# A mixer's weighted values on GpSimd in place of VectorE, in a two-layer diffusion backbone

## Chip and metric

The kernel runs on one core of a Trainium2 chip. The metric is the device time of one execution in microseconds (us), median of several runs. Profiles are of one execution each.

## The reference

Two layers of a backbone work on 512 latent and 256 context rows of width 1024. Each layer is a half-step SwiGLU feed-forward sublayer, a mixer, and another feed-forward sublayer. The mixer has Fourier channel groups and four bidirectional mLSTM heads. What matters here is how a head's states are made from its values, once for each direction:

```python
def mlstm_states(k, v, ig, lf, state0):
    ...
    a = b_tot[..., None] - b + igc
    m_loc = jnp.max(a, axis=-1)
    w = jnp.exp(a - m_loc[..., None])
    c_loc = jnp.einsum("bhcsd,bhcse->bhcde", vc * w[..., None], kc)
    n_loc = jnp.einsum("bhcs,bhcse->bhce", w, kc)

    def step(carry, xs):
        ...
        c_new = dec[..., None, None] * c_st + inj[..., None, None] * cl
        n_new = dec[..., None] * n_st + inj[..., None] * nl
```

`vc * w[..., None]` is the product that the change is about: 128 rows x 6 chunks x 129 columns (128 values and a column of ones that carries `n_loc`), for each head and each direction.

## The kernel before

Every engine has its own instruction stream, written out by hand in the block of that engine (`block.tensor`, `block.scalar`, `block.vector`, `block.gpsimd`, `block.sync`), and the streams meet only at semaphores (`S[...]`). The order on an engine is the order of the code. Matrix products with float32 data are split into a high and a low part; `split_w` makes them from each weight slot, the high part on ScalarE (L1387), the low part on VectorE (L1744).

The program runs six sublayers in a row: feed-forward, mixer, feed-forward for layer 0 and the same for layer 1. Mixer m (0 and 1) first projects its input and prepares gates; meanwhile GpSimd folds the Fourier inputs of four heads (`fold`, L1298 to L1322) and then has nothing to do until the next feed-forward sublayer (`rebuild`, L1335, then `sums`, L1348 to L1353). Then the four heads follow one another. For head h:

- TensorE (`mixer_pe`) projects q, k, k by token and v by token (`project`, L997 and L1001), does part of the Fourier products (`transform`, L1106), the products of q and k (`likeness`, L1031), and for h > 0 the transposes of the head before (`head_out`, L904). Then come the maxima (L1017, L1019), `added(h, 0)` (L1044), the Fourier products `dft` (L1088, L1091), `added(h, 1)`, the maxima of the other direction, and `inter` and `intra` (L1055, L1068) of both. `added(h, d)` multiplies k by the weighted values `wv[:, d]`, five chunks, and waits for `wv_sb`.
- ScalarE (`mixer_act`) copies the projections out of PSUM (L595); the last copy writes `vtok`, the values by token. Its semaphore is `qkv_sb`. In head 0 of each mixer it then makes the high part of a weight slot (`split(8)`, L1387). For h > 0 it takes the standard deviations of the head before (L614), which VectorE waits for in `normed`.
- VectorE (`mixer_dve`): for h > 0 it normalises the head before (`normed`, L856 and L858), which releases `head_out`. Then it makes the two weighted values (`values`, L784). Then `mixed` (L867) for the head before, or in head 0 the low part of the weight slot (L1744). Then `states(h, 0)` (L795, five steps, waits for `added(h, 0)`), `scores` (L809), `states(h, 1)`, `scores`, then `gather` and `combine` (L819 to L850), the last of which signals `hvar`.

`wv` (two directions of 6 x 129 columns) shares its memory with `num`, in which `gather` and `combine` work (`num = wv`, L395). The head's weights `wst` are ready before head 0 (semaphore `g_w`); the column of ones in `vtok` is written before it too (`nm_sel` comes behind it).

The stream of the heads on VectorE:

```python
            for h in range(HEADS):
                if h:
                    normed(h - 1)
                values(h, 0)
                values(h, 1)
                if h:
                    mixed(h - 1)
                else:
                    split(8)
                states(h, 0)
```

Of the kernel before, what the change touches and what calls it, by code (L numbers as in the profile page):

```python
# [24 lines left out]
ALU = mybir.AluOpType  # L25
# [3 lines left out]
P = 128  # L29
# [4 lines left out]
NT, NTL = TOK // P, SEQ // P  # L34
# [3 lines left out]
HEADS, HD = 4, 128  # L38
# [7 lines left out]
HV = HD + 1  # L46
# [134 lines left out]
def build(nc, x_in, w_ada0, w_ada_t, c_row_in, w_ff_in, w_ff_out, w_in, w_gates, w_out, w_qkv, cvec_in, gate_b_in,  # L181
          b_col_in, nw_col_in, nw_out_in, convw_in, convb_in, hn_w_in, fmix_in, dft_l_in, dft_c_in, dft_g_in, tri_in, x_out, gate_out_rows, nm_store, out):
    ctx = ExitStack()
    with ctx:
# [173 lines left out]
        def small(n, which="gate", end=A_DFTG):  # L358
            place[which] += n
            assert place[which] <= end  # L360
            return at(place[which] - n, n)
# [22 lines left out]
        wi, em, wst = (small(48).rearrange("p (d t h) -> p d t h", d=2, t=NT) for _ in range(3))  # L384

        def head(n):
            return small(n, "head", XN)
# [3 lines left out]
        vtok = head(NT * HV).rearrange("p (t n) -> p t n", t=NT)  # L391
        wv = head(2 * NT * HV).rearrange("p (d t n) -> p d t n", d=2, t=NT)
# [13 lines left out]
        S = {}  # L406
# [240 lines left out]
        def mixer_dve(dve, own, sub, split_w, first_out):  # L647

            m, n0, l = sub["mix"], sub["slot"], sub["l"]
# [6 lines left out]
            def split(s):  # L656
                split_w(n0 + s, (n0 + s) % 2, KC * 16 if s == 2 else SLOT)
# [119 lines left out]
            split(7)  # L777
            gates_arg()

            def values(h, d):  # L780

                if d == 0:
                    dve.wait_ge(S["qkv_sb"], 4 * (4 * m + h) + 4)
                nc.vector.tensor_tensor(wv[:, d], vtok, wst[:, d, :, h].unsqueeze(2).to_broadcast([P, NT, HV]), ALU.mult).then_inc(S["wv_sb"], 1)  # L784

            def states(h, d):

                md = 2 * (4 * m + h) + d
                if h:

                    dve.wait_ge(S["io_mm"], md - 1)
                dve.wait_ge(S["cloc_mm"], md + 1)
                for k in range(NT - 1):
                    col = scan_col(d, k, h)
                    ins = nc.vector.scalar_tensor_tensor(out=cst[:, d, k + 1, :], in0=cst[:, d, k, :], scalar=dec[:, col:col + 1],  # L795
                                                         in1=ps[:, 4 + k // 3, (k % 3) * HV:(k % 3 + 1) * HV],
                                                         op0=ALU.mult, op1=ALU.add)
                    if k < NT - 2:
                        link(ins)
                ins.then_inc(S["cst_sb"], 1)  # L800
# [52 lines left out]
            def normed(h):  # L853

                dve.wait_ge(S["hstd"], 4 * m + h + 1)
                link(nc.vector.reciprocal(den[:, 0, 1, 0:n_out], den[:, 0, 0, 0:n_out]))  # L856
                for t in range(n_out):
                    ins = nc.vector.tensor_scalar(hsum(h)[:, t, :], hsum(h)[:, t, :], mv[:, t, 0:1], den[:, 0, 1, t:t + 1], ALU.subtract, ALU.mult)  # L858
                ins.then_inc(S["hn"], 1)

            def mixed(h):

                dve.wait_ge(S["hnT"], 4 * m + h + 1)
                for g in range(2):
                    w = sub["groups"][g] * P
                    mg = mixT[:, g, 4 + h, 0:w]
                    ins = nc.vector.scalar_tensor_tensor(out=mg, in0=ps[:, 6 + g, 0:w], scalar=hn_w[:, l, h:h + 1], in1=mg,  # L867
                                                         op0=ALU.mult, op1=ALU.mult)
                ins.then_inc(S["mix_done"], 1)
# [6 lines left out]
            for h in range(HEADS):  # L876
                if h:
                    normed(h - 1)
                values(h, 0)
                values(h, 1)  # L880
                if h:
                    mixed(h - 1)
                else:
                    split(8)
                states(h, 0)
                scores(h, 0)
                if h == HEADS - 1:
                    first_out(sub)
                states(h, 1)
                scores(h, 1)  # L890
                gather(h, 0)
                gather(h, 1)
                combine(h)
# [376 lines left out]
        def _(pool):  # L1270
# [8 lines left out]
            def fold(sub, h):  # L1279
# [44 lines left out]
                steps.wait()  # L1324
                pool.sem_inc(S["folded"], 1)

            adds = Count(pool, S["s_add"])

            def rebuild(sub):
# [31 lines left out]
            for sub in SUBS:  # L1361
                if sub["kind"] == "ffn":
                    par0 = sub["slot"] % 2
                    rebuild(sub)
                    sums(sub, 0, par0, first=True)
                    sums(sub, 1, 1 - par0, second=True)
                    with adds.loop(ST // 2 - 1, 4) as i:
                        for s in range(2):
                            sums(sub, i * 2 + (2 + s), (par0 + s) % 2)
                if sub["kind"] == "mix":  # L1370
                    for h in range(HEADS):
                        fold(sub, h)


        @block.scalar
# [1062 lines left out]
```

## Time and profile before

| | us |
|---|---|
| three timed runs: median | 2498.82 |
| lowest, highest | 2495.97, 2498.97 |
| span of the profiled execution, first to last instruction | 2494.0 |
| TensorE busy in it | 2427.1 (97%) |
| VectorE busy | 1874.1 (75%) |
| ScalarE busy | 1126.9 (45%) |
| GpSimd busy | 611.6 (25%) |

The profiled execution's own time is known as its span; the timed median lies 4.8 us above it. The granted TensorE clock was 0.997 of full speed over the span. The heads of the first mixer lie at about 688 to 795 us of the span, those of the second at about 1990 to 2077. In the rows PE is TensorE, DVE VectorE, ACT ScalarE, POOL GpSimd. A row of a timeline gives the start and the length of a run of like instructions (xN of them), and in brackets how long the engine had been idle before and what ended that. `arena` is one large buffer, in which `vtok`, `wv`, `wt`, `cst` and others are pieces; `ps` is PSUM.

### The profile page before, as it was taken

The page shows a single profiled execution, that of the slowest core. Times are in us where ns is not written, and L with a number is a line of the kernel's source. Part 1 is how long each engine was busy: PE and PEld are TensorE (multiplying, and loading weights), DVE is VectorE, ACT ScalarE, POOL GpSimd, SP SyncE. Part 2 cuts the span into 40 slices and gives each one's busy share as a digit, 9 for nine tenths or more (in the row PEclk, how much of TensorE's full clock was granted, in tenths as well). Part 3 has the DMA queues.
Part 4 walks back from the last instruction along what each step waited for, and adds up shares of the span by engine and source line. Part 5 has one row for each costly group of instructions (what it writes and reads, how often), then busy time and mean ns, then how long its engine had stood idle before and what let it go on. Part 6 is the DMA issues. An engine that isn't in the chain of part 4 may idle for free.

```text
span 2494.0 us, 35459 instructions
## 1 busy us (share of the span) xinstructions
PE 2427.1 (97%) x13552; PEld 2208.6 (89%) x13552; DVE 1874.1 (75%) x2362; ACT 1126.9 (45%) x1627; POOL 611.6 (25%) x429
## 2 busy tenths in 40 slices
PE   7999999999999999999999999999999998899998
PEld 4999998888977899999888999999889777899987
DVE  5799997776567779988766799876556677898733
ACT  5334443444453743443354544443444555555522
POOL 0344440000500034544000145541000500266400
PEclk9999999999999999999999999999999999999999
DMA  6333336543111343333643423346443203322331
GB/s 258 110 127 127 140 135 256 186 148 94 52 48 36 118 160 122 129 111 132 247 161 135 169 110 126 130 156 242 180 142 101 89 28 118 136 101 101 119 118 67
DMA packets 100369, 328.33 MB, mean 132 GB/s; under 512 B 7810, under 2 KB 38050, under 8 KB 86946
## 3 DMA queue, kind: packets, MB, share of 16 engines
q1 hardware_dynamic: 83040, 316.33, 35.5%
q10 hardware_dynamic: 17218, 10.55, 1.4%
q8 instruction: 68, 1.11, 0.2%
q14 instruction: 43, 0.34, 0.0%
HBM read 318.28 MB, written 8.57 MB: 131 GB/s over the span
## 4 chain that ended last, share of the span: by engine, by line
PE 78%; DVE 12%; issue 5%; ACT 3%; DMA 2%; POOL 0%; SPq 0%; ACTq 0%; DVEq 0%; POOLq 0%
PE ps L2206 29%; PE ps L2166 27%; PE ps L2154 8%; PE ps L928 6%; DVE junk L1764 3%; DVE w_all L2014 2%; DMA acc<-w_ada_t 1%; DVE w_all L1744 1%; PE ps L2248 1%; PE ps L997 1%; PE ps L1068 1%; PE ps L1044 1%; PE ps L2258 1%; PE ps L952 1%; PE ps L1055 1%
## 5 line engine op out<-in xcount | busy, mean ns | idle before, releaser
L2206 PE MATMUL ps<-w_all,hj_all 128*128 128x512 f32 x2856 | 655.6, 391 | 4.9 <-DVE arena L828 2.5
L2206 PEld LDWEIGHTS ps<-w_all,hj_all 128*128 128x128 f32 x2856 | 535.1, 188 | 117.9 <-DVE arena L828 2.9
L2166 PE MATMUL ps<-xn_hi,w_all 128*128 128x384 f32 (+1 forms) x2592 | 612.2, 318 | 12.0 <-DVE gate_row L2067 11.1
L1744 DVE TENSOR_TENSOR w_all<-raw,w_all 128x2048 fp32r<-128x2048 f32 x138 | 322.0, 2333 | 268.8 <-ACT w_all L1387 268.7
L2166 PEld LDWEIGHTS ps<-xn_hi,w_all 128*128 128x128 f32 x2592 | 449.3, 189 | 18.9 <-DVE gate_row L2067 18.0
L2166 PE MATMUL ps<-xn_lo,w_all 128*128 128x384 f32 (+1 forms) x1296 | 411.0, 317 | 0.0
L1387 ACT ACTIVATE w_all<-raw 128x2048 fp32r<-128x2048 f32 x139 | 262.6, 1889 | 241.4 <-PE ps L2206 206.1
L2014 DVE TENSOR_TENSOR w_all<-raw,w_all 128x1024 fp32r<-128x1024 f32 (+1 forms) x216 | 329.9, 1529 | 36.5 <-ACT w_all L1609 36.2
L1764 DVE SCALAR_TENSOR_TENSOR junk<-acc,silu_row 128x1024 bf16<-128x1024 f32 x224 | 325.7, 1454 | 16.4 <-DMA acc<-w_ada_t 7.1
L1609 ACT ACTIVATE w_all<-raw 128x1024 fp32r<-128x1024 f32 (+1 forms) x216 | 197.9, 918 | 261.1 <-PE ps L2166 241.9
L2154 PE MATMUL ps<-xn_hi,w_all 128*128 128x384 f32 (+1 forms) x1024 | 245.7, 324 | 9.9 <-DVE xn_lo L1822 7.6
L2166 PEld LDWEIGHTS ps<-xn_lo,w_all 128*128 128x128 f32 x1296 | 245.1, 189 | 0.0
L2166 PE MATMUL ps<-t,w_all 128*128 128x384 f32 x1296 | 233.3, 334 | 0.0
L2166 PEld LDWEIGHTS ps<-t,w_all 128*128 128x128 f32 x1296 | 225.4, 188 | 0.0
L1613 ACT ACTIVATE gate_row<-ps 128x384 f32<-128x384 f32 (+1 forms) x216 | 100.3, 464 | 262.0 <-PE ps L2166 262.0
L2154 PEld LDWEIGHTS ps<-xn_hi,w_all 128*128 128x128 f32 x1024 | 180.2, 190 | 11.3 <-DVE xn_lo L1822 7.8
L1335 POOL TENSOR_TENSOR arena<-xn_hi,xn_lo 128x1536 f32<-128x1536 f32 (+1 forms) x8 | 27.7, 3488 | 637.5 <-DVE xn_lo L1822 637.5
L1348 POOL TENSOR_TENSOR w_sum<-raw 128x512 f32<-128x512 f32 x68 | 103.2, 1518 | 286.3 <-DMA raw<-w_ff_in 206.2
L1353 POOL TENSOR_TENSOR raw<-raw,w_sum 128x512 f32<-128x512 f32 x68 | 134.1, 1971 | 147.4 <-DVE w_all L2014 147.0
L928 PE MATMUL ps<-xn_hi,w_all 128*128 128x384 f32 (+1 forms) x640 | 165.1, 349 | 2.9 <-DVE xn_lo L1822 2.9
L2154 PE MATMUL ps<-xn_lo,w_all 128*128 128x384 f32 (+1 forms) x512 | 165.1, 322 | 0.0
L2166 PE MATMUL ps<-hj_all,w_all 128*128 128x384 f32 (+1 forms) x864 | 149.9, 321 | 2.3 <-ACT gate_row L1613 2.3
(236 smaller groups left out, 3213.0 us busy)
## 6 DMA issues: line engine op xcount, KB each, us to landing
raw<-w_ff_in SPq DMA_DIRECT2D x104, 1024.0 KB, 4.9
raw<-w_ff_out SPq DMA_DIRECT2D x77, 1024.0 KB, 5.0
acc<-w_ada_t SPq DMA_DIRECT2D x128, 512.0 KB, 3.3
raw<-w_out SPq DMA_DIRECT2D x16, 1024.0 KB, 4.9
raw<-w_in SPq DMA_DIRECT2D x12, 1024.0 KB, 5.7
x<-x_in SPq DMA_DIRECT2D x12, 512.0 KB, 10.7
gate_row<-gate_out_rows ACTq DMA_DIRECT2D x12, 512.0 KB, 6.4
x_out<-x SPq DMA_DIRECT2D x12, 512.0 KB, 9.0
```

Of the source, the lines that this page charges most:

```text
L928: ins = mm(ps[:, ch if ch < 4 else ch % 3 + 3 * g, 0:wd], w[:, k, c * P:(c + 1) * P], xx[:, k, g * GW:g * GW + wd], start=(k == 0 and i == ...
L1348: adds.link(nc.gpsimd.tensor_tensor(s21[:, 1, :], a21, a22, ALU.add))
L1353: nc.gpsimd.tensor_tensor(a12, a12, s21[:, 0, :], ALU.subtract).then_inc(S["s_sum"], 1)
L1387: nc.scalar.activation(w_hi[par][:, 0:width], raw[par][:, 0:width], ACT.Copy).then_inc(S["w_hi"], 1)
L1609: ins = nc.scalar.activation(pair_out(par0, i, 0), pair_raw(par0, i, raw[r], first), ACT.Copy)
L1613: nc.scalar.activation(fast_tmp(sub, i), ps[:, bank_, 0:sub["wide"]], ACT.Copy).then_inc(S["snap"], 1)
L1744: nc.vector.tensor_tensor(w_lo[par][:, 0:width], raw[par][:, 0:width], w_hi[par][:, 0:width].bitcast(F32), ALU.subtract).then_inc(S["w_lo" ...
L1764: ins = nc.vector.scalar_tensor_tensor(out=junk[:], in0=acc[:].rearrange("p a n -> p (a n)"), scalar=1.0, in1=silu_row[:, s, :], op0=ALU.m ...
L2014: ins = nc.vector.tensor_tensor(pair_out(par0, i, 1), pair_raw(par0, i, raw[r], first), pair_out(par0, i, 0).bitcast(F32), ALU.subtract)
L2154: ins = mm(ps[:, 4 * b + part + c, col:col + wd], w[:, k, c, :], xx[:, k, t0:t0 + wd], start=(k == 0 and i == 0), stop=(k == KC - 1 and i ...
L2166: ins = mm(ps[:, bank_, 0:xx[0].shape[-1]], w[:, c], x_[:, k, :], start=start and k == 0 and a == 0, stop=k == 3 and a == 2, skip_group_ch ...
L2206: ins = mm(ps[:, 2 * i + hf, :], xx[:, i * P:(i + 1) * P], w[:, c, hf * 512:(hf + 1) * 512], start=first and c == 0 and a == 0, stop=last ...
```

## The change

The two products of each head are taken out of VectorE's stream and put into GpSimd's, behind the four folds of the mixer. GpSimd waits once for `nm_sel` and `g_w`, and for each head for the values (`qkv_sb`) and, from the second head on, for `hvar` of the head before, since `num` and `wv` are the same memory. The arithmetic, the order on the other engines and the memory are unchanged.

```diff
--- before.py
+++ after.py
@@ -777,12 +777,6 @@
             split(7)
             gates_arg()
 
-            def values(h, d):
-
-                if d == 0:
-                    dve.wait_ge(S["qkv_sb"], 4 * (4 * m + h) + 4)
-                nc.vector.tensor_tensor(wv[:, d], vtok, wst[:, d, :, h].unsqueeze(2).to_broadcast([P, NT, HV]), ALU.mult).then_inc(S["wv_sb"], 1)
-
             def states(h, d):
 
                 md = 2 * (4 * m + h) + d
@@ -876,8 +870,6 @@
             for h in range(HEADS):
                 if h:
                     normed(h - 1)
-                values(h, 0)
-                values(h, 1)
                 if h:
                     mixed(h - 1)
                 else:
@@ -1324,6 +1316,15 @@
                 steps.wait()
                 pool.sem_inc(S["folded"], 1)
 
+            def values(sub, h, d):
+
+                k = 4 * sub["mix"] + h
+                if d == 0:
+                    pool.wait_ge(S["qkv_sb"], 4 * k + 4)
+                    if k:
+                        pool.wait_ge(S["hvar"], k)
+                nc.gpsimd.tensor_tensor(wv[:, d], vtok, wst[:, d, :, h].unsqueeze(2).to_broadcast([P, NT, HV]), ALU.mult).then_inc(S["wv_sb"], 1)
+
             adds = Count(pool, S["s_add"])
 
             def rebuild(sub):
@@ -1370,6 +1371,11 @@
                 if sub["kind"] == "mix":
                     for h in range(HEADS):
                         fold(sub, h)
+                    pool.wait_ge(S["nm_sel"], sub["mix"] + 1)
+                    pool.wait_ge(S["g_w"], sub["mix"] + 1)
+                    for h in range(HEADS):
+                        values(sub, h, 0)
+                        values(sub, h, 1)
 
 
         @block.scalar
```

On VectorE at a later head of the first mixer stood (s_hnT is signalled by the transposes of the head before, s_cloc_mm by `added`):

```order
L850 BN_AGGR arena<-arena 128x2 x5
L856 RECIPROCAL arena<-arena 128x6 [waits s_hstd]
L858 TENSOR_SCALAR arena<-arena 128x128 [waits s_dve]
L858 TENSOR_SCALAR arena<-arena 128x128 x5
L784 TENSOR_TENSOR arena<-arena 128x774 [waits s_qkv_sb]
L784 TENSOR_TENSOR arena<-arena 128x774
L867 SCALAR_TENSOR_TENSOR arena<-ps,hn_w,arena 128x384 [waits s_hnT]
L867 SCALAR_TENSOR_TENSOR arena<-ps,hn_w,arena 128x384
L795 SCALAR_TENSOR_TENSOR arena<-arena,ps 128x129 [waits s_cloc_mm,s_io_mm]
```

and now stands (line numbers of the changed kernel, L850 and L852 being `normed`, L861 `mixed`, L789 `states`):

```order
L844 BN_AGGR arena<-arena 128x2 x5
L850 RECIPROCAL arena<-arena 128x6 [waits s_hstd]
L852 TENSOR_SCALAR arena<-arena 128x128 [waits s_dve]
L852 TENSOR_SCALAR arena<-arena 128x128 x5
L861 SCALAR_TENSOR_TENSOR arena<-ps,hn_w,arena 128x384 [waits s_hnT]
L861 SCALAR_TENSOR_TENSOR arena<-ps,hn_w,arena 128x384
L789 SCALAR_TENSOR_TENSOR arena<-arena,ps 128x129 [waits s_cloc_mm,s_io_mm]
```

The two rows of 774 columns between `normed` and `mixed` are gone; nothing else moved.

On GpSimd, between the last fold of the first mixer (L1318 to L1322) and the `rebuild` of the next feed-forward sublayer stood:

```order
L1318 TENSOR_TENSOR junk<-arena 128x127 [waits s_fold]
L1320 TENSOR_TENSOR arena<-arena 128x127 [waits s_fold]
L1322 COPY arena<-junk 128x127 [waits s_fold]
L1335 TENSOR_TENSOR arena<-xn_hi,xn_lo 128x1536 [waits s_fold,s_xn_done]
L1335 TENSOR_TENSOR arena<-xn_hi,xn_lo 128x1536
L1348 TENSOR_TENSOR arena<-raw 128x512 [waits s_w_raw1]
```

and now stands (L1310 to L1314 is the end of the last fold, L1326 the products of heads 0 and 1, and then those of heads 2 and 3, which read like those of head 1):

```order
L1310 TENSOR_TENSOR junk<-arena 128x127 [waits s_fold]
L1312 TENSOR_TENSOR arena<-arena 128x127 [waits s_fold]
L1314 COPY arena<-junk 128x127 [waits s_fold]
L1326 TENSOR_TENSOR arena<-arena 128x774 [waits s_fold,s_qkv_sb,s_g_w,s_nm_sel]
L1326 TENSOR_TENSOR arena<-arena 128x774
L1326 TENSOR_TENSOR arena<-arena 128x774 [waits s_hvar,s_qkv_sb]
L1326 TENSOR_TENSOR arena<-arena 128x774
...
L1336 TENSOR_TENSOR arena<-xn_hi,xn_lo 128x1536 [waits s_xn_done]
L1336 TENSOR_TENSOR arena<-xn_hi,xn_lo 128x1536
```

Eight products of each mixer stand there now, each head's pair behind one wait of its own.

## Rows read from the trace of the kernel before

**Rows 1.** The page, part 4: the chain that ended last, by engine.
```profile
PE 78%; DVE 12%; issue 5%; ACT 3%; DMA 2%; POOL 0%; SPq 0%; ACTq 0%; DVEq 0%; POOLq 0%
```

**Rows 2.** Timeline, first mixer, head 0: start us, us, engine, line [idle before <-releaser].
```profile
697.85 1.91 ACT L1387 ACTIVATE w_all<-raw 128x2048 fp32r<-128x2048 f32 x1
...
698.06 1.84 DVE L784 TENSOR_TENSOR arena<-arena 128x774 f32<-128x774 f32 x2 [9.59 <-ACT arena L595]
699.82 2.28 DVE L1744 TENSOR_TENSOR w_all<-raw,w_all 128x2048 fp32r<-128x2048 f32 x1
...
699.48 1.38 PE L1044 MATMUL ps<-arena 128*128 128x129 f32 x10
...
702.43 1.03 PE L1091 MATMUL ps<-arena 128*128 128x256 f32 x4
704.05 1.35 PE L1044 MATMUL ps<-arena 128*128 128x129 f32 x10 [0.59 <-DVE arena L795]
```

**Rows 3.** Timeline, first mixer, head 1.
```profile
719.73 1.61 ACT L595 ACTIVATE arena<-ps 128x384 f32<-128x384 f32 x4
...
720.08 1.63 DVE L858 TENSOR_SCALAR arena<-arena 128x128 f32<-128x128 f32 x6
...
725.28 0.73 DVE L795 SCALAR_TENSOR_TENSOR arena<-arena,ps 128x129 f32<-128x129 f32 x2 [0.77 <-PE ps L1044]
...
721.86 0.84 PE L904 MATMUL ps<-ident,arena 128*128 128x128 f32 x6 [0.34 <-DVE arena L858]
...
723.79 1.38 PE L1044 MATMUL ps<-arena 128*128 128x129 f32 x10
...
727.60 1.28 PE L1044 MATMUL ps<-arena 128*128 128x129 f32 x10
```

**Rows 4.** Timeline, first mixer: from a ScalarE evacuation to GpSimd's first fold.
```profile
626.12 0.87 ACT L515 ACTIVATE arena<-ps 128x384 f32<-128x384 f32 x2 [6.37 <-PE ps L928]
...
627.06 0.45 POOL L1298 TENSOR_TENSOR junk<-arena 128x127 f32<-128x127 f32 x1 [259.11 <-ACT arena L515]
```

**Rows 5.** Timeline, second mixer, head 1.
```profile
2016.81 1.63 ACT L595 ACTIVATE arena<-ps 128x384 f32<-128x384 f32 x4
...
2017.15 1.12 DVE L858 TENSOR_SCALAR arena<-arena 128x128 f32<-128x128 f32 x4
...
2020.23 0.87 DVE L867 SCALAR_TENSOR_TENSOR arena<-ps,hn_w,arena 128x256 f32<-128x256 f32 x2
```

**Rows 6.** Chain in order of time, second mixer, head 1: start us, us, what.
```profile
2019.98 1.33 PE ps L1044 x10
...
2021.40 0.36 DVE arena L795
...
2023.43 1.35 PE ps L1044 x10
```

**Rows 7.** GpSimd's tensor_tensor by line: duration ns min/median/max.
```profile
L1299 POOL TENSOR_TENSOR junk<-arena x8: 410/778/2457, 627.5 to 1974.0; 128x127 f32<-128x127 f32 x8
L1348 POOL TENSOR_TENSOR w_sum<-raw x68: 1282/1295/2378, 116.5 to 2342.0; 128x512 f32<-128x512 f32 x68
L1358 POOL TENSOR_TENSOR w_all<-raw,w_all x1: 4502/4502/4502, 38.3 to 38.3; 128x2048 fp32r<-128x2048 f32 x1
```

**Rows 8.** Timeline: GpSimd and VectorE at work at the same time, at two places.
```profile
1061.32 1.28 POOL L1349 TENSOR_TENSOR raw<-raw 128x512 f32<-128x512 f32 x1
1062.57 2.27 POOL L1350 TENSOR_TENSOR w_sum<-w_sum,raw 128x512 f32<-128x512 f32 x1
...
1061.36 2.33 DVE L2014 TENSOR_TENSOR w_all<-raw,w_all 128x1024 fp32r<-128x1024 f32 x1 [0.62 <-ACT w_all L1609]
...
1977.79 2.49 POOL L1309 TENSOR_TENSOR arena<-junk 128x127 f32<-128x127 f32 x4
...
1979.77 0.58 DVE L744 TENSOR_SCALAR arena<-arena 64x128 f32<-64x128 f32 x1
1980.39 0.28 DVE L745 TENSOR_SCALAR arena<-arena 64x128 f32<-64x128 f32 x1
```

## Prediction

> **What bounds the kernel now.** I read the page's chain first [rows 1]. TensorE carries 78% of it, VectorE 12%, GpSimd nothing. So time taken off VectorE counts only where TensorE waits for it, and I went on to the operation that moves. It is L784, 16 times by the code: a pair in each of four heads in each of two mixers. A pair takes 1.84 us [rows 2], so 14.7 us (8 x 1.84) is the most that the change could give. Then I read the timeline around three places: the first head of the first mixer [rows 2], a later head of it [rows 3], a later head of the second mixer [rows 5, 6]. The reader is to look there for who is waited for at the end of each wait.
>
> In a later head of the first mixer ScalarE ends its four copies of k and v at 721.34 (719.73 + 1.61) [rows 3]. VectorE finishes the six L858 at 721.71, does the pair of products, then L867, and then sits idle 0.77 us until TensorE's L1044 releases L795 at 725.28. So VectorE has spare time right behind the products. TensorE starts L1044, the reader of the first product, at 723.79 with no wait before it, and reads the second product only at 727.60. In the second mixer the same L795 waits too: L867 ends at 2021.10 (2020.23 + 0.87) [rows 5] and the chain runs from L1044 at 2019.98 to L795 at 2021.40 and back to L1044 at 2023.43 [rows 6]. There the chain passes the reader of the first product with nothing to spare on its way to the states.
>
> **What leaving VectorE gives.** In six of the eight heads (all but the first of each mixer) L867 moves up to when its transposes are done, and L795 then waits longer for TensorE. L867 was in time before, so nothing is gained. In the first head of a mixer the pair runs 698.06 to 699.90 and is followed by the split L1744 at 699.82 [rows 2]. But that split also needs ScalarE's L1387, which ends at 699.76 (697.85 + 1.91). With the pair gone it could start at about 699.80, at best 0.1 us earlier, two times. I take 0.
>
> **What a product costs on GpSimd.** No row has this shape on GpSimd. Its plain tensor_tensor took 1.282 us at best for 512 columns and 4.502 us for 2048 [rows 7]. The line through them is 0.209 us + 2.096 ns a column, so 774 columns take 1.83 us, against 0.92 on VectorE (half a pair). One input is a broadcast column and the pattern has six pieces, which may shift it. From below it can't be under the 512-column row, 1.28. From above I take the rate of the 127-column row, 0.410 us / 127 x 774 = 2.50. I take 1.83, since two rows of the same engine on both sides of 774 give it. The Trainium skill ("GPSIMD Engine Reference", section 3.1) gives about 2.6 cycles an element at 1.2 GHz: 1.68 us as an estimate without the dispatch. By it the delay below would be 1.1 us in place of 1.5.
>
> **When it starts and ends.** GpSimd's first fold started 0.07 us after ScalarE's L515 ended (626.12 + 0.87 = 626.99, then 627.06) [rows 4]. I take 0.08. From VectorE's last L858 (721.71) to TensorE's L904 it is 0.15 in [rows 3]; I use 0.14 for GpSimd too.
>
> Second mixer, later heads: the copies end at 2018.44 (2016.81 + 1.63) [rows 5]. The product runs 2018.52 to 2020.35, and TensorE can start at 2020.49. It started at 2019.98 [rows 6]. That is 0.51 late, on the chain, for heads 1, 2 and 3: **+1.5 us**. The second product ends at 2022.2 and is read at 2023.43, so it is hidden with 1.1 to spare. L795 waits 0.51 longer too, so the loss passes whole to the next L1044.
>
> First mixer, later heads: copies end 721.34, the product would start 721.42, while the last L858 is still running until 721.71. Suppose it is held off until then (see the lock below): it ends at 721.71 + 1.83 - 0.13 = 723.41, TensorE can go at 723.55, and it went at 723.79 [rows 3]. **0**, with 0.24 to spare. The second ends near 725.2, read at 727.60. **0**.
>
> First head of both mixers: VectorE's pair started 698.06, so GpSimd's first product runs about 698.05 to 699.88. TensorE's L1044 then starts at 700.02 in place of 699.48, and the Fourier products behind it (L1088, L1091), which ended at 703.46, move by no more than that, to 704.0. That is still ahead of the L1044 at 704.05, which waits 0.59 for L795 anyway [rows 2]. The split L1744 comes at 699.80 and meets GpSimd's last columns; the second product waits behind it to 702.1 and ends at 702.10 + 1.70 = 703.80, readable at 703.94 against 704.05. **0 to +0.1 each**, I take 0.
>
> The added waits on GpSimd stand in front of the `rebuild` of the next feed-forward sublayer alone, which waits for rows made after the mixer's output product, so nobody is held up behind them. No DMA moves, and SyncE's queue is untouched.
>
> **The lock.** The trace shows that the two engines exclude each other. GpSimd's 512-column operation at 1061.32 took its plain 1.28; VectorE's split of 0.04 us later took 2.33, ending 1.09 after it; the next GpSimd operation, at 1062.57, took 2.27, ending 1.15 after the split [rows 8]. The second to come waits for the first to end, and hides 0.13 of its own start. Single-input operations are in it too: L744 took 0.58 with GpSimd's L1309 running, and L745, of the same shape, 0.28 when it was over [rows 8]. The Trainium skill ("SBUF — State Buffer", section "Who interferes with whom") states it as an exclusive lock in which issue order decides who blocks, and counts tensor_scalar from memory to memory and two-input operations among those that take it; by that rule, L858 and L1744 contend and L867, L795 and L809 (one input in PSUM) don't. The trace agrees as far as those rows go.
>
> **Sum.** 0 (VectorE's relief) + 0 (first mixer) + 1.5 (second mixer) = +1.5 us on a span of 2494.0. The timed median of the runs is 2498.82, 4.8 us above the span; I add the 1.5 to it: 2500.3.
>
> **Rivals.**
> 1. *GpSimd wins the lock over the split in the first head.* Its second product is issued about 0.05 before its first ends (1062.57 against 1062.60 shows 0.03), so at 699.83 to 699.85, and the split comes at 699.80 to 699.82. If the product comes first it runs to 701.67 and the split ends at 701.67 + 2.15 = 703.82 in place of 702.10: +1.7 twice, total +4.9, 2503.7. A product a few hundredths shorter than 1.83 decides it. At the lower end, 1.28, the split would end at 702.7 and the whole be +1.2. Chance 0.14.
> 2. *Slower: GpSimd comes between the L858.* The six start about 0.26 apart, the last at 721.37 (721.71 - 0.34). GpSimd asks at 721.42. If it is served ahead of the sixth (it decides if the copies' signal arrives 0.05 us earlier, or if the sixth asks only when the fifth has ended at 721.45), the sixth ends at 721.42 + 1.83 + 0.21 = 723.46, 1.75 late. TensorE's transposes L904 wait for it on the chain, three times: +5.2, total +6.7, 2505.5. In the second mixer the four L858 end at 2018.27, ahead of the copies, so it doesn't occur. Chance 0.12.
> 3. *The product is slow on GpSimd,* at 2.50: second mixer 1.18 x 3, first mixer 0.43 x 3, first heads 2 x 1.1: +7.0, 2505.8. The total passes 5 us at about 2.3 us a product. Chance 0.06.
> 4. *Faster:* the relief of VectorE counts after all, because TensorE's next work waits on VectorE by something the chain put on another engine. At most 14.7. Idle time right after the pair in every head I looked at speaks against it. Chance 0.03.
> 5. *My forecast,* +0.5 to +3: 0.60. No change at all, because the product is 1.3 us long or the slack is larger: 0.05.
>
> **How the numbers follow.** About 0.2% (5.0 us here) is what a measurement can tell from no change. Over it lie rival 2 (0.12), half of rival 3 (0.03) and a third of rival 1, which stands at 4.9 (0.04): slower 0.18 or so. Faster 0.03. The rest, 0.79, is no change. The three timed runs lie 3.0 us apart, so I put 1.5 below and above. Low 2497: no change at all less noise. High 2506: rivals 1 and 2 with it, and most of 3.
>
> **What would show it.** L784's successor appears on GpSimd 16 times, median near 1.83 (1.7 to 2.0; more where the lock held it). TensorE idles about 0.5 us ahead of its first added products in the second mixer, released by GpSimd, and not in heads 1 to 3 of the first. The time from head to head stays in the first mixer and grows by 0.5 us in the second. Wrong would be: a L858 of 2 us; the split L1744 of a first head taking 4 us; or a head's period getting shorter.

## The result and the profile after

| | median us | runs | ratio to the kernel before, 95% interval |
|---|---|---|---|
| before | 2498.89 | 4 | |
| changed | 2510.51 (2505.99 to 2514.59) | 4 | 1.0051 [1.0037, 1.0065] |

The change costs 0.5%, 11.6 us. The forecast was 2500.3, with 2506 as its upper end. It was wrong in size and in the likeliest case: two collisions that it had given small chances both happened, and the clock, which no case had, fell.

The profiled execution took 2512.26 us; its span is 2510.3, 16.3 us more than that of before. Its page (busy times, chain by engine) reads:

```profile
PE 2437.0 (97%) x13552; PEld 2217.6 (88%) x13552; DVE 1866.8 (74%) x2346; ACT 1126.6 (45%) x1627; POOL 634.1 (25%) x445
...
PE 77%; DVE 12%; issue 5%; ACT 3%; DMA 2%; POOL 0%; SPq 0%; DVEq 0%; ACTq 0%; POOLq 0%
```

The chain looks as it did [rows 1]. VectorE lost only 7.3 us of busy time (1874.1 before) though 14.7 us of products left it, and TensorE gained 9.9 (2427.1 before) with the same 13552 matmuls. Both are signs of instructions that took longer, so I looked for those. The product itself, by its line (duration ns min/median/max), was shorter than forecast:

```profile
L1326 POOL TENSOR_TENSOR arena<-arena x16: 1483/1486/1522, 700.6 to 2072.5; 128x774 f32<-128x774 f32 x16
```

To place the loss I cut both traces at the same two events: the first L989 (L997 before) of a mixer, and the first L2212 (L2206 before) of its output product. The windows of the kernel before first, with one inner stretch that is needed below. The columns are start and end, length, busy time and count of PE, PEld (weight loads), DVE, ACT and POOL, the granted clock PEclk, DMA share and GB/s:

```profile
688.76:785.14 96.38, 92.71 (x626) 76.81 (x626) 71.64 (x180) 48.64 (x118) 0.00 (x0) 1.00 0.09 32
767.47:770.47 3.00, 2.66 (x20) 1.98 (x18) 3.00 (x8) 2.30 (x4) 0.00 (x0) 1.00 0.00 0
1990.60:2068.80 78.20, 74.16 (x500) 61.08 (x501) 58.74 (x162) 41.31 (x94) 0.00 (x0) 1.00 0.11 39
```

And the changed kernel, with four inner stretches:

```profile
core 0: us, PE busy (x) PEld busy (x) DVE busy (x) ACT busy (x) POOL busy (x), PEclk, DMA share, GB/s
691.25:795.55 104.30, 96.02 (x626) 79.30 (x626) 69.93 (x172) 48.63 (x118) 11.83 (x8) 0.97 0.09 29
775.00:778.00 3.00, 1.47 (x9) 0.98 (x9) 1.97 (x3) 1.00 (x1) 2.75 (x2) 1.00 0.00 0
778.30:784.70 6.40, 6.40 (x20) 5.32 (x21) 2.93 (x8) 1.66 (x6) 0.00 (x0) 0.50 0.00 0
2000.88:2083.50 82.62, 76.64 (x500) 63.41 (x500) 53.13 (x154) 41.30 (x94) 11.73 (x8) 0.96 0.11 37
2013.00:2017.00 4.00, 1.63 (x12) 1.26 (x11) 3.33 (x8) 0.66 (x2) 0.00 (x0) 1.00 0.41 129
2017.20:2023.80 6.60, 6.60 (x28) 5.60 (x27) 4.01 (x11) 1.14 (x4) 0.00 (x0) 0.50 0.18 71
```

The first mixer grew from 96.38 to 104.30 us, the second from 78.20 to 82.62: 12.3 us together, and the median rose by 11.6. In the profile the rest of the span grew by 4.0 more (2319.4 to 2323.4); a second profile of the same kernel (run after2 below) has 12.4 in the mixers and -0.8 outside, so those 4.0 aren't the change. Outside the mixers, too, TensorE has stretches of 3.4 us at a granted clock of 0.50: four in this profile, its start and end apart (from 358.2, 2092.2, 2126.3 and 2382.3), two in that of before (2110.1 and 2366.1), two in after2 (804.2 and 2377.7).

Three things make up nearly all of the 12.3.

**The sixth normalisation.** Timeline of the first mixer, head 1 (compare [rows 3]). The third and fourth rows are the same line in later windows, which show its last two instructions and its last one alone; the fifth shows the first product of the pair alone:

```profile
723.33 1.61 ACT L595 ACTIVATE arena<-ps 128x384 f32<-128x384 f32 x4
...
723.68 2.94 DVE L852 TENSOR_SCALAR arena<-arena 128x128 f32<-128x128 f32 x6
...
724.71 1.90 DVE L852 TENSOR_SCALAR arena<-arena 128x128 f32<-128x128 f32 x2
...
724.97 1.65 DVE L852 TENSOR_SCALAR arena<-arena 128x128 f32<-128x128 f32 x1
...
725.01 1.52 POOL L1326 TENSOR_TENSOR arena<-arena 128x774 f32<-128x774 f32 x1 [21.46 <-ACT arena L595]
...
726.76 0.85 PE L896 MATMUL ps<-ident,arena 128*128 128x128 f32 x6 [1.65 <-DVE arena L852]
```

ScalarE's copies end at 724.94 and GpSimd's product starts at 725.01. VectorE's sixth L852 is on record from 724.97, 0.04 earlier, and yet it takes 1.65 us where the others take 0.34, and ends 0.09 after the first product (726.53). The fifth, begun at 724.71, runs until 725.05, past the product's start, and the product takes 1.52 us where the products that meet nothing take 1.483 to 1.491. So it reads as if the product waited those 0.03 to 0.04 for the fifth to end and was served then, ahead of the sixth. It is the same in all fifteen heads of the five profiles in which the sixth took 1.65 (products of 1.515 to 1.522 us); no run shows the engines' requests themselves. TensorE's L896 waits 1.65 us in place of 0.34. The six at 748.57 and 773.45 show the same 2.94. A head lasts 24.88 us from one L852 to the next in place of 23.57. That is +1.31 three times, 3.9 us.

**The split of slot 8.** Timeline of the first heads of both mixers (compare [rows 2]); the last row is the kernel before, second mixer:

```profile
700.34 1.91 ACT L1393 ACTIVATE w_all<-raw 128x2048 fp32r<-128x2048 f32 x1
...
702.07 1.49 POOL L1326 TENSOR_TENSOR arena<-arena 128x774 f32<-128x774 f32 x1
...
702.34 3.37 DVE L1750 TENSOR_TENSOR w_all<-raw,w_all 128x2048 fp32r<-128x2048 f32 x1 [11.37 <-ACT w_all L1393]
...
707.65 1.35 PE L1036 MATMUL ps<-arena 128*128 128x129 f32 x10 [1.51 <-DVE arena L789]
...
2015.95 1.43 PE L1036 MATMUL ps<-arena 128*128 128x129 f32 x10 [2.37 <-DVE arena L789]
...
2004.51 1.35 PE L1044 MATMUL ps<-arena 128*128 128x129 f32 x10 [1.85 <-DVE arena L795]
```

In the second mixer the split took 3.42 us. In the first the second product starts at 702.07, when the split L1750 isn't ready, as ScalarE's L1393 ends at 702.25. VectorE gets going at 702.34 and the split takes 3.37 us in place of 2.28. From the mixer's start to this L1036 it is 16.40 us (707.65 - 691.25) in place of 15.29, and 15.07 in place of 13.91 in the second mixer: +1.1 and +1.2.

**TensorE's clock.** The windows show what no case of the forecast had: 6.4 us at a granted clock of 0.50, which is 1.2 GHz where 1.00 is 2.4, in the fourth head of the first mixer, and 6.6 us in the second mixer behind its L1036. Ahead of them TensorE was busy 1.47 of 3.00 us and 1.63 of 4.00. In the kernel before it was busy 2.66 of 3.00 us at the place that answers to the first (767.47, the same distance ahead of its L904), and 2.15 of 4.00 at the place that answers to the second (2001.56), with a granted clock of 1.00 at both. Its matmuls in the slow stretch of the first mixer:

```profile
778.72 2.52 PE L1036 MATMUL ps<-arena 128*128 128x129 f32 x10
781.03 3.62 PE L1080 MATMUL ps<-arena 128*128 128x256 f32 x8
```

In the other heads these two take 1.38 and 1.89, so 2.87 us less. What the clock cost can be read from the matmuls' starts. From the fourth head's L896 (776.53) to its second L1036 (785.53) it is 9.00 us, and 5.76 in the heads at full clock: 3.24 us. In the second mixer it is 16.74 us from the late L1036 (2015.95) to the next L896 (2032.69), and 13.90 between the same two in the kernel before (2004.51, 2018.41): 2.84 us.

In the second mixer, heads 1 to 3 are 19.15 us long in place of 18.99. The chain there (start us, us, what), against [rows 6]:

```profile
2032.79 1.50 POOL arena L1326
...
2034.34 1.40 PE ps L1036 x10
```

TensorE follows the product's end by 0.04. So 82.62 - 78.20 = 4.42 is 0.5 for these three heads, 1.2 for the split and 2.8 for the clock, to within 0.1.

One small gain stands against this. At the end of the first mixer, VectorE sits idle before its last L828, the last operation ahead of the output product. In the kernel before:

```profile
784.06 1.03 DVE L828 TENSOR_TENSOR arena<-arena,ps 128x387 f32<-128x387 f32 x2 [0.78 <-PE ps L1068]
```

In the changed kernel its idle time there is 0.41 in place of 0.78, and the output product starts 0.37 us sooner. The same 0.41 stands in every other run below but b_early, also in b_delay and b_delay2, whose products are on VectorE; so it isn't the product's leaving that did it. What did wasn't traced.

The whole: 3.9 + 2.3 + 0.5 + 6.1 - 0.4 = 12.4 of the 12.3, with each term read on its own.

### The profile page after: what moved, and what is told of

Same layout as the page of the kernel before. It is cut to its first block, busy times and chain, and to the rows that moved or that the text cites. A ratio compares the mean times of both kernels' runs of the same rounds, so it can differ in the third digit from the quotient of the medians.

```text
span 2510.3 us, 35466 instructions
## 1 busy us (share of the span) xinstructions
PE 2437.0 (97%) x13552; PEld 2217.6 (88%) x13552; DVE 1866.8 (74%) x2346; ACT 1126.6 (45%) x1627; POOL 634.1 (25%) x445
## 4 chain that ended last, share of the span: by engine, by line
PE 77%; DVE 12%; issue 5%; ACT 3%; DMA 2%; POOL 0%; SPq 0%; DVEq 0%; ACTq 0%; POOLq 0%
PE ps L2212 29%; PE ps L2172 27%; PE ps L2160 8%; PE ps L920 6%; DVE junk L1770 3%; DVE w_all L2020 2%; DVE w_all L1750 1%; DMA acc<-w_ada_t 1%; PE ps L2254 1%; PE ps L989 1%; PE ps L1036 1%; PE ps L1060 1%; PE ps L1047 1%; PE ps L944 1%; ACT w_all L1393 1%
## 5 line engine op out<-in xcount | busy, mean ns | idle before, releaser
L2212 PE MATMUL ps<-w_all,hj_all 128*128 128x512 f32 x2856 | 657.1, 391 | 4.6 <-DVE arena L822 2.2
L2212 PEld LDWEIGHTS ps<-w_all,hj_all 128*128 128x128 f32 x2856 | 536.4, 189 | 117.8 <-DVE arena L822 2.5
L1750 DVE TENSOR_TENSOR w_all<-raw,w_all 128x2048 fp32r<-128x2048 f32 x138 | 324.0, 2348 | 291.1 <-ACT w_all L1393 291.0
L1393 ACT ACTIVATE w_all<-raw 128x2048 fp32r<-128x2048 f32 x139 | 262.6, 1889 | 243.8 <-PE ps L2212 202.5
```

Source lines behind the costliest of these rows:

```text
L1393: nc.scalar.activation(w_hi[par][:, 0:width], raw[par][:, 0:width], ACT.Copy).then_inc(S["w_hi"], 1)
L1750: nc.vector.tensor_tensor(w_lo[par][:, 0:width], raw[par][:, 0:width], w_hi[par][:, 0:width].bitcast(F32), ALU.subtract).then_inc(S["w_lo" ...
L2212: ins = mm(ps[:, 2 * i + hf, :], xx[:, i * P:(i + 1) * P], w[:, c, hf * 512:(hf + 1) * 512], start=first and c == 0 and a == 0, stop=last ...
```

## The experiments

Two questions were open: are the two collisions the cause, and is the slow clock their consequence or an accident? All ratios are to the kernel before on the same chip.

**a_hn.** GpSimd waits for the normalisations.

```
             if k:
                 pool.wait_ge(S["hvar"], k)
+                if h:
+                    pool.wait_ge(S["hn"], k)
```

> The changed kernel, with one more wait on GpSimd: from head 1 on, a product starts only when VectorE has normed the head before (its six L852 instructions are through), so that it can't come between them. Theory A (the two engines contend for the pair of ports, and TensorE's clock falls as a consequence of its longer waits): the six take 1.63 us again in place of 2.94, the first mixer's heads last 23.6 to 24.1 us in place of 24.9, the granted clock at the fourth head of the first mixer is 1.00 in place of 0.50 at the 7 us around 778 us, so the first mixer shrinks from 104.3 us to 97.5 to 99; the second mixer stays at 82.6 with its slow clock; in all 4 to 7 us below the changed kernel, near 2505. Rival B (the clock falls for a reason that has nothing to do with the product's place): the six are short again, but a stretch at 0.50 stays in the first mixer, which lasts 100 to 101. Rival C (the product's own 1.49 us on GpSimd against VectorE's is what costs): the heads stay at 24.9, since the product now even starts later.

Measured: 2502.28 us, ratio 1.0022 [1.0012, 1.0032], by the ratios some 7 us under the changed kernel. Timeline of head 1, then the window of the first mixer (columns as above):

```profile
719.75 1.63 DVE L852 TENSOR_SCALAR arena<-arena 128x128 f32<-128x128 f32 x6
...
721.52 0.85 PE L896 MATMUL ps<-ident,arena 128*128 128x128 f32 x6 [0.34 <-DVE arena L852]
...
721.55 2.93 POOL L1328 TENSOR_TENSOR arena<-arena 128x774 f32<-128x774 f32 x2 [21.93 <-DVE arena L852]
```

```profile
687.32:784.44 97.12, 92.77 (x626) 76.80 (x626) 66.02 (x172) 48.69 (x118) 11.73 (x8) 1.00 0.09 31
```

The six take 1.63 again, L896 waits 0.34, the heads last 23.57, and the clock in the first mixer is 1.00. The mixer, at 97.12 just under the 97.5 to 99 expected, is 7.2 us shorter, of which 3.9 are the six and 3.2 the clock. The product starts 0.17 after their end and is still in time. Theory A held, rivals B and C fell here. The second mixer, where nothing was changed, again lasted 82.62 us and kept its slow stretch, 6.4 us at 0.50 from 2008.2.

**a_split.** The second product of head 0 waits for the split.

```
+        if h == 0 and d:
+            pool.wait_ge(S["w_lo"], sub["slot"] + 8 + 1 + START)
         nc.gpsimd.tensor_tensor(wv[:, d], vtok, wst[...]..., ALU.mult)
```

> The changed kernel, with one more wait on GpSimd: in head 0 of each mixer the second product starts only when VectorE's split of slot 8 (L1750) is written. Theory A: L1750 takes 2.3 us again in place of 3.4, TensorE's wait at L1036 falls back from 1.51 to 0.6 us in the first mixer and from 2.37 to 1.9 in the second, 0.9 to 1.1 us a mixer; if the slow clock in the second mixer (0.50 at 2017 to 2024 us) is a consequence of that longer wait, it goes too, and the second mixer shrinks from 82.6 to 78.5 to 79.5 us; the first mixer's heads 1 to 3 stay as they are, with the slow clock at 778 us. In all 2 to 5 us below the changed kernel. Rival B: the slow clock in the second mixer stays, and that mixer lasts 81.5. Rival C: the late second product (near 2 us later) holds back what reads it, and nothing is gained.

Measured: 2504.33 us, 1.0033 [1.002, 1.0046]. Timeline of the first mixer's head 0, then windows of both mixers:

```profile
702.31 1.49 POOL L1328 TENSOR_TENSOR arena<-arena 128x774 f32<-128x774 f32 x1 [2.60 <-DVE w_all L1752]
...
699.94 2.29 DVE L1752 TENSOR_TENSOR w_all<-raw,w_all 128x2048 fp32r<-128x2048 f32 x1 [11.37 <-ACT w_all L1395]
...
704.18 1.35 PE L1036 MATMUL ps<-arena 128*128 128x129 f32 x10 [0.43 <-DVE arena L789]
```

```profile
688.86:790.48 101.62, 94.41 (x626) 78.27 (x626) 68.86 (x172) 48.63 (x118) 11.87 (x8) 0.98 0.09 30
1997.92:2076.61 78.69, 73.79 (x501) 60.87 (x501) 51.87 (x154) 41.30 (x94) 11.77 (x8) 1.00 0.11 38
```

The split is back at 2.29 us, TensorE waits 0.43 in place of 1.51 although the product now starts 2.6 us after the first one ended. The second mixer is 3.9 us shorter, 1.2 of it the split and 2.8 the clock, which stays at 1.00. In the first mixer the waits of 1.65 us remain, and so does a slow stretch, a shorter one (0.50 from 775.4 to 778.4; 101.62 is 1.6 us over the 96.06 of the run a_both below and the 3.9 of the six). The same kernel once more, one execution:

> The kernel whose second product of head 0 waits for the split, once more, for one look at the clock. Theory A: the waits of 1.65 us at L896 bring a stretch at 0.50 into the first mixer again (101.5 to 103.5 us), none into the second, which stays at 78.7. Rival B: the first mixer at 100 us, with 1.00, or the second with 0.50.

Measured: 2505.01 us, mixers of 101.62 and 78.68 us, a stretch of 0.50 again in the first (at 751 us this time), none in the second. Theory A.

**a_both.** Both waits.

> The changed kernel with both waits of the two runs before it: no product lies beside the split of head 0, none between the six normalisations. Theory A: the effects add, no stretch at 0.50 is left within either mixer; first mixer 96.4 to 98.5 us against 96.4 of the kernel before and 104.3 of the changed one, second 78.2 to 79.5 against 78.2 and 82.6; total 2499 to 2502, within 0.15% of the kernel before. Rival B: slow stretches stay in the mixers, 2503 to 2506. Rival C: 2508 or more.

Measured: 2495.20 us, 0.9992 [0.9983, 1.0001]. Windows of both mixers:

```profile
687.93:783.99 96.06, 92.78 (x627) 76.81 (x627) 64.93 (x172) 48.63 (x118) 11.76 (x8) 1.00 0.10 32
1989.42:2068.09 78.67, 73.79 (x500) 60.86 (x501) 51.87 (x154) 41.30 (x94) 11.77 (x8) 1.00 0.11 38
```

The mixers sum to 174.73 us against 174.58 of before: the whole loss is gone, with the products still on GpSimd. (The second is 0.5 longer, the first 0.3 shorter, by the 0.37 at its end told above.) The median lies 2.2 us under that of before and under the 2499 to 2502 that I expected, which the mixers don't explain and the interval doesn't confirm. The second mixer's 0.5 is the price of the GpSimd product, as forecast in kind.

**a_fill.** The collisions stay, TensorE gets work in its waits.

```
     if h:
         pe.wait_ge(S["xab_sb"], k + 1)
+        if m == 0:
+            for _ in range(4):
+                mm(ps[:, 6, 0:GW], kT[:, 0:P], qT[:, 0:GW], start=True, stop=True)
         head_out(pe, sub, h - 1)
...
     dft(h)
+    if h == 0:
+        pe.wait_ge(S["wt_sb"], 8 * m + 1)
+        for _ in range(4):
+            mm(ps[:, 2, 0:GW], kT[:, 0:P], qT[:, 0:GW], start=True, stop=True)
     added(h, 1)
```

> The changed kernel; on TensorE four matmuls of some 1.3 us in all, whose result nobody reads, stand in two of its waits: ahead of the head's output in the first mixer's heads 1 to 3, and ahead of L1036's wait in head 0 of both mixers. The collisions on VectorE stay (L852 2.94 us, L1750 3.4 us). Theory A: TensorE idles less before the places where the clock fell, so the granted clock stays at 1.00 at 778 us and at 2017 us and the matmuls L1036, L1080 and L1047 take 1.4, 1.9 and 1.2 us again; each mixer shortens by up to 2.9 us less what the extra matmuls add on the path (0 to 1.3 us each head), in all 0 to 5 us below the changed kernel. Rival B: the stretches at 0.50 stay where they were and the time rises by what the matmuls add.

Measured: 2508.97 us, 1.0053 [1.004, 1.0066]. Timeline of the two collisions, then windows of both mixers:

```profile
725.16 2.94 DVE L852 TENSOR_SCALAR arena<-arena 128x128 f32<-128x128 f32 x6
...
2011.72 3.42 DVE L1757 TENSOR_TENSOR w_all<-raw,w_all 128x2048 fp32r<-128x2048 f32 x1 [9.78 <-ACT w_all L1400]
```

```profile
691.89:796.00 104.11, 102.30 (x659) 82.74 (x659) 69.94 (x172) 48.69 (x118) 11.83 (x8) 1.00 0.08 29
2002.01:2081.82 79.81, 76.15 (x509) 62.39 (x509) 53.01 (x154) 41.34 (x94) 11.73 (x8) 1.00 0.11 38
```

The collisions are unchanged (2.94 and 3.42), but the clock is 1.00 in both mixers. In the second, where the extra matmuls fit into the wait, the mixer is 2.8 us shorter: the price of the clock by a second way. In the first they don't fit; each later head grew from 24.88 to 25.62 us, and the mixer stayed where it was, within 0.2. The median says as little: 11.6 us over the kernel before, as the changed kernel, though the mixers' windows come to 9.3. So this was no gain in time, but it separates the clock from the collisions.

**after2.** The changed kernel again, beside the runs that follow.

> The changed kernel once more, unaltered, on the same chip as the runs beside it. Theory A (the slow clock within the mixers follows from this kernel's waits): the profile shows 0.50 again in the fourth head of the first mixer or close to it, and in head 0 of the second; mixers of 104.3 and 82.6 us within 0.5. Rival B (the clock falls by chance): the stretches lie elsewhere or are gone, 101.4 and 79.8 us. Time within 2507 to 2513 in either case.

Measured: 2508.93 us, 1.0046 [1.0033, 1.0059]; mixers 104.28 and 82.67; 0.50 at 749.8 to 756.2 us (the third head this time, not the fourth) and at 2016.1 to 2022.5. The slow stretches recur with the same sum; only the head varies.

**b_delay.** The kernel before, no product on GpSimd, but VectorE late.

```
+    def spend():
+        nc.vector.tensor_tensor(gate_row[:, 1, :], silu_row[:, 0, :], silu_row[:, 1, :], ALU.mult)
     def normed(h):
         dve.wait_ge(S["hstd"], 4 * m + h + 1)
+        if m == 0 and h < HEADS - 1:
+            spend()
...
     else:
+        spend()
         split(8)
```

> The kernel before, all products on VectorE and GpSimd idle, with one more VectorE operation of 2 x 1024 values (some 1.2 us, its result isn't read) ahead of the six normalisations in the first mixer's heads 1 to 3 and ahead of the split of slot 8 in head 0 of both mixers. It gives TensorE waits as long as the collisions did, without GpSimd. Theory A (the clock falls because TensorE waits longer): TensorE's wait at L904 is 1.5 to 1.6 us in place of 0.34, each of these heads lasts 1.2 us longer, and stretches at a granted clock of 0.50 appear in the first mixer and in head 0 of the second: mixers of 103 to 105 and 82 to 82.5 us, time 2507 to 2512. Rival B (the clock falls for another reason, as power drawn by GpSimd beside VectorE): it stays 1.00 in the mixers, which last 101.0 to 101.5 and 79.2 to 79.6 us, time 2503 to 2505.

Measured: 2504.53 us, 1.0026 [1.0016, 1.0036]. Timeline of two waits, one in each mixer, then windows of both mixers and of a stretch in the second:

```profile
722.94 0.85 PE L911 MATMUL ps<-ident,arena 128*128 128x128 f32 x6 [1.48 <-DVE arena L864]
...
2008.28 2.49 PE L1051 MATMUL ps<-arena 128*128 128x129 f32 x10 [2.99 <-DVE arena L795]
```

```profile
687.57:788.12 100.55, 92.72 (x627) 76.80 (x627) 76.17 (x184) 48.69 (x118) 0.00 (x0) 1.00 0.09 30
1993.23:2076.71 83.48, 78.34 (x500) 64.94 (x500) 60.05 (x163) 41.34 (x94) 0.00 (x0) 0.94 0.11 36
2008.00:2017.40 9.40, 9.12 (x38) 8.06 (x39) 4.81 (x14) 1.14 (x4) 0.00 (x0) 0.50 0.28 107
```

Mixed. In the second mixer the longer wait (2.99 us at the line that waited 1.85) brings 9.4 us at 0.50, with GpSimd idle: its work isn't needed for it. In the first mixer three waits of 1.47 to 1.48 us and one of 1.72 in head 0 did not, and it lasted 100.55. My expectation of a slow stretch there was a miss, and so was that of the time, 2507 to 2512.

**b_delay2.** The same in the first mixer alone, with two such operations in each later head, one behind the other.

> The kernel before, products on VectorE and GpSimd idle, with two more VectorE operations of 1024 values ahead of the six normalisations in the first mixer's heads 1 to 4 (the fourth one falls in the tail) and nothing added in head 0. TensorE's wait at L904 becomes 0.34 + 2 x 1.2 = 2.8 us. Theory A (long waits of TensorE bring the slow clock, with or without GpSimd; 1.47 us did not suffice in the first mixer, 1.65 did): each of these heads lasts 26.0 to 26.2 us and at least one stretch at 0.50 lies in the first mixer, which lasts 96.4 + 7.4 + 1.5 to 6, so 105 to 110 us; the second mixer stays at 78.2 with a clock of 1.00. Rival B (the clock needs GpSimd's work beside VectorE's): 1.00 throughout the first mixer, 103.5 to 104.

Measured: 2514.99 us, 1.0060 [1.0036, 1.0084]. The wait in head 1 of the first mixer, then windows of both mixers and of one inner stretch:

```profile
725.40 0.85 PE L911 MATMUL ps<-ident,arena 128*128 128x128 f32 x6 [2.86 <-DVE arena L865]
```

```profile
689.79:803.74 113.95, 103.09 (x626) 84.35 (x626) 79.10 (x186) 48.68 (x118) 0.00 (x0) 0.90 0.08 27
726.70:733.10 6.40, 6.40 (x20) 5.06 (x20) 3.82 (x10) 1.66 (x6) 0.00 (x0) 0.50 0.00 0
2011.12:2089.32 78.20, 74.15 (x501) 61.08 (x501) 58.77 (x162) 41.34 (x94) 0.00 (x0) 1.00 0.12 39
```

Each of the three waits of 2.86 us is followed by a stretch at 0.50 (the second from 754.0 to 763.8, the third from 784.7 to 791.1), and the second mixer, left alone, is again 78.20 us at 1.00. The first grew by 17.6 us where the waits add 7.6; the rest, some 10, is the clock. Theory A's 105 to 110 was too low, as I had counted on fewer slow stretches.

**b_early.** The split itself: can it leave this place? With the products on VectorE as before, ScalarE does its part of the split of slot 8 after the second of its head's four copies, VectorE ahead of the head's products.

```
 ScalarE:   project(h, 1)
+           if h == 0: split(8)
            ...
            project(h, 3)
-           if h == 0: split(8)
 VectorE:  +split(8)
            dve.wait_ge(S["g_w"], m + 1)
            for h in range(HEADS):
                ...
-               else: split(8)
```

> The kernel before, with the split of slot 8 moved ahead in both mixers: ScalarE copies the high part before it evacuates slot 0's product pair of head 0 (where it idles 1.3 us), VectorE takes its own part ahead of head 0's products (where it idles 9.6 us). Nothing else is changed. Theory A (this split is what TensorE waits for behind L795): TensorE's waits at L1044 of head 0, 0.59 and 1.85 us, go to 0 to 0.6; first mixer 95.7 to 96.4 us against 96.4, second 76.4 to 77.7 against 78.2 (ScalarE's evacuations there come up to 1 us later); 1 to 2.4 us below the kernel before. Rival B: ScalarE's later evacuations cost what is gained, no difference.

Measured: 2496.02 us, 0.9994 [0.9985, 1.0003]. The split in the first mixer and TensorE's wait in the second, then windows of both mixers:

```profile
694.09 2.29 DVE L1743 TENSOR_TENSOR w_all<-raw,w_all 128x2048 fp32r<-128x2048 f32 x1 [6.29 <-ACT w_all L1386]
...
2003.10 1.35 PE L1043 MATMUL ps<-arena 128*128 128x129 f32 x10 [0.34 <-DVE arena L795]
```

```profile
688.08:783.73 95.65, 92.55 (x627) 76.97 (x627) 71.82 (x180) 48.59 (x118) 0.00 (x0) 1.00 0.09 32
1990.70:2067.40 76.70, 74.14 (x500) 61.07 (x501) 58.94 (x162) 41.12 (x94) 0.00 (x0) 1.00 0.11 39
```

The split runs while VectorE would be idle, TensorE waits 0.34 in place of 1.85 in the second mixer and not at all in the first. The mixers lose 0.7 and 1.5 us, 2.2 in all. The median fell by 1.6, within what can be told from nothing.

**a_early.** The same with the products on GpSimd, with a_hn's wait; neither collision can happen.

> The changed kernel (products on GpSimd) with the wait behind the six normalisations from head 1 on, and the split of slot 8 moved ahead as in the run beside it, so that neither collision can happen. Theory A: the products on GpSimd are then hidden in the first mixer and cost 0.15 us a head in the second; mixers of 95.5 to 96.3 and 76.8 to 78.2 us, no stretch at 0.50 in them, time within 1 us of the run that has the early split with the products on VectorE, 2495 to 2499. Rival B: 1.49 us a product on GpSimd against 0.92 on VectorE shows in head 0, where TensorE waits for both, and this version is 1 to 2 us above the other.

Measured: 2495.73 us, 0.9991 [0.9982, 0.9999]. The first mixer lasted 95.44 us; the window of the second:

```profile
1991.08:2068.93 77.85, 73.78 (x501) 60.87 (x501) 51.91 (x154) 41.08 (x94) 11.72 (x8) 1.00 0.12 39
```

As fast as the run before it; both medians lie under that of the kernel before by what can hardly be told from nothing. In the mixers' windows the two versions with the early split are 2.2 and 1.3 us shorter than the kernel before, wherever the product stands. They differ by GpSimd's price in the second mixer (77.85 against 76.70): 0.5 in heads 1 to 3, as before, and 0.6 in head 0, where TensorE's first L1035 waits 0.84 us for GpSimd, and waited 0.20 for VectorE.

## Why the prediction was wrong

- **Relief of VectorE worth nothing: right.** a_both, with all products gone from VectorE and no collision, has the mixers of before within 0.2 us: 0.5 for GpSimd's product in the second, less the 0.37 at the end of the first, which isn't the relief.
- **The product's cost: direction right, size off.** 1.49 us against 1.83. The line through two rows of other shapes was 0.34 too high. The lower estimate from the Trainium skill ("GPSIMD Engine Reference", section 3.1), 1.68, was nearer, also too high. The signal to TensorE took 0.04, not 0.14.
- **Second mixer, heads 1 to 3: right in kind.** Forecast +0.51 each, measured +0.16 (19.15 against 18.99), mostly the shorter product's doing. The prediction also took TensorE's start of L1044 from the chain, 2019.98, where the timeline has the first of the ten matmuls at 2019.91; so its own delay was 0.58 and not 0.51. That less 0.34 (product) and 0.10 (signal) leaves 0.14 of the 0.16.
- **First mixer, heads 1 to 3 at 0: the step that failed first.** The text said "suppose it is held off until then", that is that GpSimd's request comes after the sixth normalisation holds the ports. Rival 2 named the other case and its condition: the sixth asks only when the fifth has ended. The trace fits that. The sixth is on record 0.04 before GpSimd's start, but the fifth was then still running (to 725.05), and the sixth lost. The text supposed a hold until the sixth's end, 721.71; what the records fit is a hold until the fifth's. The price was put at 1.75 a head and was 1.31, again by the shorter product. A chance of 0.12 for it was too low: the row of the kernel before already had the six 0.26 apart and 0.34 long, so each was on record before its predecessor had ended, and which of the two times counts was open. The Trainium skill ("SBUF — State Buffer", section "Who interferes with whom") says that issue order decides; the order on record does not tell it when two operations of an engine overlap.
- **Head 0 at 0: failed too.** Rival 1 happened, in both mixers. It said that a product a few hundredths shorter than 1.83 decides it; it was 0.34 shorter, so the second product began 0.27 before the split. Price forecast 1.7 each, measured 1.1 to 1.2. The two rivals shared one cause, GpSimd asking a little earlier than VectorE, and I gave each a small chance of its own and none to both. By the forecast's own prices both together come to 1.5 + 3.4 + 5.2 = 10.1 us, 2508.9, past the end of the range. Its signs of being wrong, a L858 of 2 us and a split of 4, came smaller, at 1.65 and 3.4, by the same shorter product.
- **What no case had: the clock, a term put at nothing without a reason.** With rivals 1 and 2 together and my own +0.5, the measured prices give 3.9 + 2.3 + 0.5 = 6.7 us, about 2505.5, inside the range. That this lies in the range is the shorter product's doing. The rest is the granted clock, 6.1 us, less the 0.4 at the end of the first mixer; the clock is what carried the time out of the range. That it follows from TensorE's waits is shown from three sides: it goes in the mixer whose collision goes (a_hn in the first, a_split in the second, a_both in both), it goes when the collisions stay and the waits are filled (a_fill), and it comes without GpSimd when VectorE is late (b_delay in the second mixer, b_delay2 in the first). What isn't settled is where it sets in. The length of one wait isn't the measure: 1.65 us at L896 brought it in four profiles of four (the changed kernel and a_split, twice each), in the third or the fourth head, while 1.72 at b_delay's first L1051 and 1.85 at the L1044 of the kernel before (2004.51 in the second mixer) did not.

The profiles are of one execution each. In the timed executions the slow clock shows in their mean granted clock, median 0.993 in the five of after2 and 0.996 in the 29 of the kernel before beside them, and by the sum: changes in the mixers' windows from one profile each against changes of the median are 12.3 and 11.6 (changed kernel), 5.2 and 4.9 (a_hn), 5.7 and 6.9 (a_split), 9.3 and 11.6 (a_fill), 9.5 and 6.9 (b_delay), 17.6 and 17.3 (b_delay2).

## What to carry to other kernels

When work moves to GpSimd, list what VectorE does at the moment at which the new operation is released, not only whether GpSimd is free; a product of 1.5 us that slips between two short operations costs nearly its whole length (1.31 us here), and one more wait on GpSimd for VectorE's signal took that back (a_hn; a second such wait, at the split, the rest: a_both). Price a new wait of TensorE with the granted clock: look in the windows at what it was busy ahead of each stretch, and reckon that a wait added to a stage which already has some can cost more than its own length. An experiment that fills the wait with matmuls that nobody reads separates the two costs.

## What the runs showed of the hardware

- Of two VectorE operations back to back, the second can be on record before the first has ended, and still be held up by a GpSimd operation that starts 0.04 us later: 1.65 us for a 0.34 us tensor_scalar of 128 columns. The GpSimd operation itself took 1.52 us in place of 1.49 there, by which it waited for the first to end.
- A GpSimd product of 774 columns with one broadcast operand took 1.483 to 1.522 us, 1.92 ns a column, less than the 2.50 (1.282 us for 512) and 2.20 (4.502 us for 2048) of its plain rows [rows 7].
- Waits of TensorE of 1.65 to 3 us, with other shorter ones near them, were followed by 3 to 10 us at a granted clock of 0.50. A stretch of 6.4 to 6.6 us was worth 2.8 and 3.2 us where it could be separated. Single waits of 1.72 and 1.85 us were not followed by one, and stretches of 3.4 us lie outside the mixers in the kernel before too.
